# The first expert pack runs through to its down products before the second pack's rows are turned

## What is computed

```python
def moe(h, router_w, router_b, w_gate, w_up, w_down):
    ...
    gates = jnp.sum(jax.nn.one_hot(idx, N_EXPERTS, dtype=F32) * w[..., None], axis=1)
    hg = jnp.einsum('td,edf->tef', t, w_gate)
    hu = jnp.einsum('td,edf->tef', t, w_up)
    act = jax.nn.silu(hg) * hu * gates[..., None].astype(t.dtype)
    out = jnp.einsum('tef,efd->td', act, w_down)
    return out.reshape(shp)
```

## Time and profile before

| | |
|---|---|
| median of 3 runs | 1600.3 us (1597.43 to 1601.24) |
| profiled execution, time | 1603.66 us |
| profiled execution, span | 1601.8 us |
| mean granted TensorE clock | 0.971 |
| PE busy | 1465.1 us, 91% |
| VectorE busy | 589.1 us, 37% |
| ScalarE busy | 561.5 us, 35% |
| GpSimd busy | 180.3 us, 11% |
| gate/up products (L959) | 199.8 us in both layers |
| down products (L980) | 103.7 us in both layers |
| row turnings (L943) | 32.6 us in both layers |
| act turnings (L968) | 11.0 us in both layers |

### The profile page before, as it was taken

The page is one execution under the profiler, slowest core; times in us unless marked ns, Lnnn a source line. Parts: engine busy times, 40 slices in busy tenths (PEclk is TensorE's granted clock), DMA queues, the critical chain, the costliest instruction groups (busy, mean ns, idle before and its releaser), DMA issues.

```text
span 1601.8 us, 19000 instructions
## 1 busy us (share of the span) xinstructions
PE 1465.1 (91%) x7515; PEld 743.2 (46%) x7515; DVE 589.1 (37%) x926; ACT 561.5 (35%) x1233; POOL 180.3 (11%) x179
## 2 busy tenths in 40 slices
PE   6999899999989999698899899899989999799980
PEld 3444444444463333564455455455454445533330
DVE  1134566663350000553454554555553033400004
ACT  4112445451112221433663673673570001122212
POOL 0112000000020000300400410410410100200002
PEclk9999999999999999799999999999899999999995
DMA  9603666579099999604232232223055021999985
GB/s 346 222 1 112 233 217 210 205 235 389 7 366 399 419 408 373 234 1 144 88 103 77 92 114 83 92 94 104 28 172 208 14 105 46 372 390 419 408 334 210
DMA packets 121331, 323.28 MB, mean 202 GB/s; under 512 B 7814, under 2 KB 37206, under 8 KB 110998
## 3 DMA queue, kind: packets, MB, share of 16 engines
q1 hardware_dynamic: 100396, 260.33, 44.0%
q0 software_dynamic: 8496, 31.17, 5.2%
q10 hardware_dynamic: 12352, 30.58, 4.9%
HBM read 279.05 MB, written 42.99 MB: 201 GB/s over the span
## 4 chain that ended last, share of the span: by engine, by line
PE 79%; DVE 8%; DMA 4%; ACT 4%; issue 3%; POOL 1%; SPq 1%; ACTq 0%; POOLq 0%; DVEq 0%
PE ps L959 12%; PE ps L1060 10%; PE ps L1220 9%; PE ps L1115 9%; PE ps L739 7%; PE ps L980 6%; PE ps L908 4%; PE ps L813 3%; PE ps L829 3%; PE ps L686 2%; PE ps L1062 2%; PE ps L1199 2%; PE ps L943 2%; PE ps L1191 1%; DVE mem L2028 1%
## 5 line engine op out<-in xcount | busy, mean ns | idle before, releaser
L959 PE MATMUL ps<-mem 128*32 128x512 f32 (+1 forms) x1408 | 199.8, 597 | 2.0 <-ACT mem L1402 2.0
L1060 PE MATMUL ps<-mem 128*128 128x512 f32 x384 | 171.5, 600 | 1.5 <-ACT mem L1592 1.5
L1220 PE MATMUL ps<-mem 128*128 128x512 f32 x320 | 140.7, 599 | 3.2 <-issue 2.7
L1115 PE MATMUL ps<-mem 128*128 128x512 f32 x320 | 142.4, 598 | 0.0
L1920 DVE TENSOR_TENSOR mem<-ps,mem 128x256 f32<-128x256 f32 x28 | 11.9, 425 | 337.5 <-ACT mem L1411 337.5
L1990 DVE SCALAR_TENSOR_TENSOR mem<-mem 128x642 f32<-128x642 f32 x96 | 92.6, 965 | 88.0 <-ACT mem L1516 85.4
L959 PEld LDWEIGHTS ps<-mem 128*32 128x32 f32 (+1 forms) x1408 | 59.4, 118 | 124.5 <-issue 124.2
L1060 PEld LDWEIGHTS ps<-mem 128*128 128x128 f32 x384 | 72.2, 193 | 83.8 <-issue 81.8
L739 PE MATMUL ps<-mem 128*128 128x512 f32 x240 | 106.4, 600 | 1.9 <-DVE mem L1694 1.9
L980 PE MATMUL ps<-mem 128*32 128x512 f32 (+1 forms) x704 | 103.7, 601 | 4.3 <-ACT mem L1415 4.3
L1552 ACT ACTIVATE mem<-mem,small 128x128 f32<-128x128 f32 x320 | 95.1, 391 | 26.7 <-DMA mem<-cum_rows 26.7
(11 more groups left out here) (318 smaller groups left out, 2029.5 us busy)
## 6 DMA issues: line engine op xcount, KB each, us to landing
mem<-in_mod_w SPq DMA_DIRECT2D x24, 2048.0 KB, 9.1
mem<-in_expert_w_gate SPq DMA_DIRECT2D x40, 1024.0 KB, 10.7
mem<-in_expert_w_up SPq DMA_DIRECT2D x40, 1024.0 KB, 13.9
mem<-in_expert_w_down SPq DMA_DIRECT2D x40, 1024.0 KB, 15.1
mem<-cum_rows SPq DMA_DIRECT2D x40, 512.0 KB, 5.3
slot_rows<-mem ACTq DMA_DIRECT2D x28, 512.0 KB, 8.1
mem<-slot_rows ACTq DMA_DIRECT2D x26, 512.0 KB, 11.1
slot_rows<-mem SPq DMA_DIRECT2D x1, 12288.0 KB, 52.8
```

The costliest lines, as they stand in the source:

```text
L959: last = nc.tensor.matmul(ps[c:c + w, 2 + j, :], XGT[j][:, k, c:c + w], GUW[l][m][:, :, k, :], start=(k == 0), stop=(k == KD - 1))
L1060: nc.tensor.matmul(ps[:, b, :], w[:, k, :], HT[:, k, SEQ:TOK], start=(k == 0), stop=(k == KD - 1))
L1115: last = nc.tensor.matmul(ps[:, ZBANK[t], :], HT[:, k, t * P:(t + 1) * P], WZ[2 * k // KD][:, k % (KD // 2), :], start=(k == 0), stop=(k = ...
L1220: last = nc.tensor.matmul(ps[:, 4 + n % 4, :], YT[b][:, k, t * P:(t + 1) * P], w[:, k, :], start=(b == 0 and k == 0), stop=(b == 1 and k = ...
```

## The change

On PE, the act turning and the down products of pack 0 are taken out of the first pass of the loop and put straight behind the gate/up products of pack 0, ahead of the wait for the scatter and of the row turning of pack 1. On ScalarE, the copy of pack 0's turned activations (`act_out`) goes ahead of the copy of pack 1's rows. The copy and store of pack 0's result (`result_out`) stay where they were on ScalarE. VectorE, GpSimd and SP are unchanged, and so is all that follows pack 1. It is done in both layers.

```diff
@@ PE
                 first_rows()
                 gate_up(d0, 0, *ring(0), first=True)
+                act_turned(d0, 0)
+                down(d0, 0, *ring(0))
                 pe.wait_ge(ES["sc"], 2 * NT * 16 * (l + 1))
                 rows_turned(d0 + 1, 1, r0[1] + 1)
                 for t in range(PACKS):
                     if 0 < t < PACKS - 1:
                         rows_turned(d0 + (t + 2), t % 2, r0[t % 2] + ((t + 2) // 2 + t % 2))
-                    act_turned(d0 + t, t % 2)
+                    if t > 0:
+                        act_turned(d0 + t, t % 2)
                     if t + 1 < PACKS:
                         gate_up(d0 + (t + 1), (t + 1) % 2, *ring(t + 1))
                     if t in (0, PACKS - 1):
                         rows_turned(d0 + (t + 2), t % 2, r0[t % 2] + ((t + 2) // 2 + t % 2))
-                    down(d0 + t, t % 2, *ring(t))
+                    if t > 0:
+                        down(d0 + t, t % 2, *ring(t))
@@ ScalarE
                 gate(d0, 0)
+                act_out(d0, 0)
                 rows_out(d0 + 1, 1)
                 load_rows(3, 1)
                 for t in range(PACKS):
                     if 0 < t < PACKS - 1:
                         rows_out(d0 + (t + 2), t % 2)
                         load_rows(t + 4, t % 2)
-                    act_out(d0 + t, t % 2)
+                    if t > 0:
+                        act_out(d0 + t, t % 2)
                     if t + 1 < PACKS:
                         gate(d0 + (t + 1), (t + 1) % 2)
```

## The result

The changed kernel is slower. Over 20 executions of each, side by side, the median is 1610.96 us against 1604.43, and the ratio is **1.0043, 95% interval 1.0024 to 1.0062**: +3.9 to +9.9 us, where 2.5 was forecast. The median of 1600.3 that the prediction starts from came from 3 executions; 20 put it 4 us higher (1596.35 to 1612.71), so the ratio is what counts. Applied to 1600.3 us it gives 1607.2, above the forecast range of 1598.5 to 1606.6.

What follows compares the result with a forecast made beforehand. PE's work bounds the kernel (79% of the chain). Layer 0 +5.46 − 2.33 = +3.13, layer 1 +3.41 − 1.70 − 2.33 = −0.62, together +2.5 us: 1600.3 to 1602.8 us, range 1598.5 to 1606.6.

Steps and rivals of the forecast that it cites:

- steps 1 and 3: Gate/up of pack 1: start put off by +5.46 us (layer 0), +3.41 (layer 1); layer 1's clock stays up, −1.70 us.
- rival (c): First products start late in both layers, so layer 1 has layer 0's +3.13: together +6.3 us, 1606.6 us; chance 0.10.
- (a): PE's clock falls in the new waits, 1.70 us a fall: one gives 1604.5, one in each layer 1606.2; chance 0.20.
- (b): Layer 0 starts early too, first rows' products 9.1 us in both layers: total −1.8, 1598.5 us; chance 0.15.
- (d): Pack 3's rows come late for their turning on PE: +1 to +3.8 us, 1603.8 to 1606.6; chance 0.07.
- What was costed at nothing: SP's later load of expert 6, pack 0's down weights, its later result, pack 3's rows: 0 us taken.

Runs made afterwards that it cites:

- the control: The kernel before, unchanged, under another name, measured against the kernel before: ratio 1.0016 (1.0000 to 1.0032), median 1605.03 us.
- the first four experiments: Against the kernel before: change in layer 0 alone 1.0021, in layer 1 alone 1.0038, kernel before unchanged 1.0016, changed kernel once more 1.0035.
- half of the change: Against the kernel before, only act turning of pack 0 and its copy go ahead, down products stay; one execution of 1603.63 us, only its pieces used.
- other order: Kernel before reordered: act turning of pack 0, rows of pack 1, down of pack 0, rows of pack 2, gate/up of pack 1; 0.9977 and 0.9980.
- with 7 matmuls: 7 in place of 4 matmuls without use ahead of the first products: old order 1.0007, changed order 1.0004, other order 0.9999.
- with 12 matmuls: 12 in place of 4 matmuls without use ahead of the first products: old order 0.9993, changed order 1.0063.

## Why the prediction was wrong

**The pieces were right.** The bare chain ahead of the down products was put at 2.13 us and took 489.11 − 487.16 = 1.95 and 1406.92 − 1404.87 = 2.05. The down products took 3.57, as said. From gate/up of pack 0 to that of pack 1 the sum has 15.04, the traces 14.89 and 14.90. From the end of gate/up of pack 1 to gate/up of pack 2 it has 3.51, the traces 505.51 − 502.00 = 3.51 and 3.45. Layer 0 was put at +3.13; against the trace before it is +2.99, and +3.27 against the control.

**The step that failed is layer 1 of steps 1 and 3**: "**+3.41 us**, less because the 2.27 us of waiting for rows disappear inside the new work", and "**−1.70 us**" for the clock. Both credits belong to a wait that the one trace had and no other profile of the old order with the usual four matmuls has: in layer 1 of the control and of the run with the change in layer 0 only, PE waits 0 us for pack 1's rows, and gate/up of pack 1 takes 7.09 us. Without the credits layer 1 costs +3.23 in place of −0.62, and the sum is 6.5 and not 2.5. That 6.5 lies so near to the measured 6.9 is in part luck, as the interval is 6 us wide.

This is rival (c), "Both start late", at +6.3 us, to which I gave 0.10 because "The profile shows one of each, which is for neither". What I had not read is how close the race was. Pack 1's rows against the end of gate/up of pack 0, in all profiles, from SP's issue of their load, its time to landing, and PE's timeline:

| profiles | stretches | rows landed, us after the end of gate/up of pack 0 |
|---|---|---|
| before | 2 | +0.1 (layer 0), **+2.2** (layer 1) |
| changed, and the first four experiments | 10 | −2.3 to −0.2 |
| half of the change, other order twice | 6 | −0.7 to +1.1 |
| with 7 matmuls | 6 | +1.6 to +2.5 |
| with 12 matmuls | 4 | −4.0 to −2.2 |

Of the 18 stretches with the usual four matmuls, the one that the credits were read from is the only one in which the rows came more than 1.1 us late. Its first products took 9.12 us, with no fallen clock and no idle pieces. A part of the reason was in the trace: there the matmuls without use ran at the lower clock, so they took 5.38 us where those of layer 0 took 3.68, and PE was idle only 1.74 us ahead of the first products, against 3.44:

```profile
456.46 3.68 PE L925 MATMUL ps<-mem,tab 128*128 128x512 f32 x8
...
1372.88 5.38 PE L925 MATMUL ps<-mem,tab 128*128 128x512 f32 x8
```

The clock was low there (0.50 from 1373.7 to 1377.0 us in the busy times by stretch) and rose in time for the products. In the control it fell at 1378.8, where the products start, and stayed low for 5.8 us:

```profile
1378.80:1384.60 5.80, 5.80 (x27) 5.80 (x28) 3.39 (x14) 0.00 (x0) 4.28 (x6) 0.50 0.94 372
```

It is only a part. Layer 1 of the changed kernel's second profile has the same 5.38 us and 1.73 us of idle time, and its first products still took 12.76 us, by idle pieces among them. Those pieces stand in the ten stretches of the table's second row and in none of the eight of the first and third, where the race is open; what they come from was not found. So the trace before could show that the outcome in layer 1 hung on 2 us, which asked for a larger chance for (c), but not how often PE is late.

**The other rivals.** (a) did not happen: in the five changed stretches of each layer gate/up of pack 1 took 7.0 us every time, as in these two stretches of the changed kernel, each from its start to gate/up of pack 2, the clock at 1.00:

```profile
494.98:505.50 10.52, 9.31 (x50) 4.55 (x50) 0.42 (x1) 2.32 (x3) 0.00 (x0) 1.00 0.50 189
1412.70:1423.10 10.40, 9.29 (x50) 4.14 (x50) 0.42 (x1) 2.33 (x3) 0.00 (x0) 1.00 0.44 166
```

At its end, behind gate/up of pack 1, each holds 3.5 us of nothing but transposes and 1.1 to 1.2 us of idle time. The rule of the Trainium skill that transposes don't bring the array to full clock (TensorE: Matmul & The Clock Gate, Part 4: PE-mode transpose) would have it fall here, and no run shows that: in the same stretch of all ten the clock stayed at 1.00. (b) was in effect made by the 7 matmuls: from the first products to gate/up of pack 2 the changed order is then 2.15 us shorter in layer 0 and level in layer 1, where (b) has −1.2 and −0.6 us; the times, 1604.46 against 1605.93, agree within their uncertainty. (d) did not happen either: pack 3's rows were asked for at 493.82, landed 7.6 us later and were wanted at 504.30. They did not come sooner than the 7.5 us before, as the prediction thought they would with SP's queue dry, though the DMA engines' share was 0.50 from 497 to 499 us and 0.03 from there to 501.

**What was costed at nothing** did cost nothing. SP asked for expert 6 only at 502.10, and the DMA engines ran half empty: the rows above read 0.50 and 0.44 in the DMA column, 5 to 6 us without work in each layer, where I had put the hole at 4.3 at most. Most of it is one piece (0.03 and 0.00 from 499 to 501 and 503 us in layer 0). Yet from gate/up of pack 2 to the first surplus pack it is 122.19 us in layer 0 and 122.27 in layer 1 in the changed kernel as before, to a hundredth. No product waited for a weight.

**The sign and the range.** The forecast called +2.5 us, no change that can be told. The interval +3.9 to +9.9 lies above it, and most of it above the 0.3% bound (4.8 us), for which the prediction had 0.19.

## What to carry to other kernels

A wait read from one execution can be spent only if other executions have it too: before crediting a stall that hangs on a race between an engine and a transfer, work out from the trace how close the race was, here 0.1 us in one layer and 2.2 us in the other, and look at a second profile. And when work is moved into a hole, look at what it was hiding where it stood: the down products left behind a 1.2 us wait for a copy, and put the whole chain of silu, multiply, turning and copy bare. An order that keeps one product beside each copy lost nothing, and perhaps gained a little.

## What I had not expected of the hardware

- The first rows' products, 80 equal matmuls, took 9.12 to 13.35 us in the same program. The clock explains up to 2.9 us of it (10.8 us after a short fall, 11.7 to 12.1 with a longer one, all without idle pieces). The rest is idle pieces of 0.2 to 0.8 us among the last 2 to 26 of them, for which the profile names nothing that was waited for ("issue"). They stand in the changed kernel, in the first four experiments and in the two late ones, and in none of the other profiles. The control has them and the first profile of the same kernel has not. The first four experiments ran on one chip, the two late ones on a second, and the six without pieces on two others, so they may go with the chip. What they are was not found.
- Starting 2.6 us or more earlier bought the old order nothing, since PE's wait for rows brought the lower clock: gate/up of pack 1 took 9.86 us and 8.54 us behind waits of 2.60 and 1.70 us, and 7.09 without them.
- The DMA engines could stand half empty for 10 us in a stage in which they are otherwise full (1.00 to 1.03 in the DMA column), and no weight came late.
